# Attention on Trainium2: a home for the turned gate in the values' PSUM bank, and another place for it in the order

## Chip, cores, metric

The kernel runs on one core of one Trainium2 chip. The metric is the device time of one launch in microseconds (us).

## What is computed

One inference step of a two-layer hybrid encoder: a prompt of 1,024 tokens, and 8 running streams of 16 tokens each with caches. Each layer projects its input, runs three attention branches side by side (A: forgetting attention with a causal mask; B: a window of 128 tokens with sinks; C: latent attention with a mask by chunks of 64), multiplies each branch by silu of its gate, projects, merges and normalises. Cut to what matters here (prompt part, one layer):

```python
oa = _swept_attention(qa, ka, va, _causal, F)          # 8 heads of 64
ob = _banded_sink_attention(qb, kb, vb, sinks)
kc, vc = _mla_keys(ckv, kpe, w_uk, w_uv)
oc = _swept_attention(qc, kc, vc, _chunk_causal)
br = stack([oa * silu(ga), ob * silu(gb), oc * silu(gc)])
up = einsum('bsnw,nwd->bsnd', br, w_br)
mixed = (sigmoid(gates) * up).sum(axis=2)
```

The change is in the prompt's attention, and in `oa * silu(ga)` (and its like for B and C) there.

## The kernel before

Each layer runs phases one after the other, with a barrier of all engines between them. The phase of this change is `prompt_attention`. It works through 12 units: 4 pairs of heads for each of the kinds a, b and c. A unit has 16 sub-steps m; sub-step m takes head m % 2 of the pair and the 128 queries of tile a = m // 2. The window of tile a has a + 1 key tiles in kinds a and c, and at most two in kind b.

For one sub-step the engines do this:

- **Score** (PE, L1438, for kind a also the mask L1442): queries by keys into the PSUM tile `ss`. DVE then takes the row's maximum (L1558), and ACT the exponential into `p` (L1509), which also sums the rows.
- **Turn** (PE, L1452): the probabilities are transposed 128 columns at a time into `tr`, a ring of two PSUM banks. Up to four transposes make one group, and a group fills one bank. A sub-step with up to four key tiles (m up to 7 in kinds a and c, every m in kind b) has one group, later ones two. DVE copies the last group of a sub-step into `pt` (L1565), ACT the first of two (L1516). Behind the copy of an odd sub-step DVE divides the gate by the row sums (L1574, L1575) and writes it to `sgr`.
- **Value** (PE, L1469), once for both heads of a tile, behind the odd sub-step: values by `pt` into the PSUM bank `oo`, which holds the two heads' 128 x 128 result.
- **Gate** (PE, L1478): `sgr` is transposed, into the same ring `tr`, as a group of its own. **Mix** (DVE): the turned gate is copied to SBUF (L1581, `sgt`), and `oo` times `sgt` goes to `o` (L1586).
- **Fill** (PE, L1488 to L1490, 24 matmuls): a piece of the projection for the merge gates, put in between; ACT evicts it (L1523).

The order is one list, written out by `attention_order`; every engine walks it and does its own part. For an even m it reads: turn m, score m + 2, gate and mix of the tile before, perhaps a fill. For an odd m: turn m, score m + 2, perhaps a fill, value. (In kind b both scores m + 2 and m + 3 stand behind the even turn.) Fills stand at all odd m and at m = 4 in kinds a and b (m = 4 only in the last unit of b), and in kind c at m = 2, 3, 4, 5, 6, 8, 10, 12 and 13. With m + 2 past 15 the score is that of the next unit.

PE runs its instructions in order. `bank_free(pe, g)` holds group g of the ring until group g - 2 has been copied out. Since the gate is a group too, the groups of an odd turn with two groups go into the banks in this way: the even turn has g and g + 1, the gate g + 2, the odd turn g + 3 and g + 4; so g + 4 waits for the copy L1581 of the gate, which stands on DVE behind the maximum of score m + 2.

Of the kernel before, what the change touches and what calls it, by code (L numbers as in the profile page):

```python
# [14 lines left out]
P = 128  # L15
# [1103 lines left out]
def attention_order():  # L1119


    order = [("score", 0, 0), ("score", 0, 1)]
    fills = [(n, t) for n in range(len(UNITS)) for t in range(NT)][EARLY_FILLS:]
    order = [("fill", *fills.pop(0)) for _ in range(3)] + order
    places = {kind: [1, 3, 5, 7, 9, 11, 13, 15, 4] if kind != "c" else [2, 3, 4, 5, 6, 8, 10, 12, 13] for kind in "abc"}
    spare = EARLY_FILLS + 3
    for n in range(len(UNITS)):
        for m in range(SUBS):
            before = None if m % 2 or m + n == 0 else (n, m // 2 - 1) if m else (n - 1, PT - 1)
            order.append(("turn", n, m))  # L1130
            n2, m2 = (n, m + 2) if m + 2 < SUBS else (n + 1, m + 2 - SUBS)
            if n2 < len(UNITS) and UNITS[n2][0] != "b":
                order.append(("score", n2, m2))
            elif n2 < len(UNITS) and m2 % 2 == 0:
                order += [("score", n2, m2), ("score", n2, m2 + 1)]
            if before:
                order += [("gate", *before), ("mix", *before)]
            if m in places[UNITS[n][0]][:len(places["a"]) - (n < spare)]:
                order.append(("fill", *fills.pop(0)))
            if m % 2:  # L1140
                order.append(("value", n, m // 2))
    order += [("gate", len(UNITS) - 1, PT - 1), ("mix", len(UNITS) - 1, PT - 1)]
    assert not fills
    return order


def prompt_attention(nc, C, T, S, l):
# [33 lines left out]
    chain = ph.sem("chain")  # L1181
    tr_made, tr_taken = ph.sem("tr_made"), ph.ring("tr_taken", 2)
    s_made, max_ready, exp_ready = ph.sem("s_made"), ph.sem("max_ready"), ph.sem("exp_ready")
    sgr_ready, pv_made, o_ready = (ph.sem(n) for n in ("sgr_ready", "pv_made", "o_ready"))
    o_stored = ph.ring("o_stored", 2)
    gw_loaded, gw_hi, gw_lo = ph.sem("gw_loaded"), ph.sem("gw_hi"), ph.sem("gw_lo")
    g_made, g_taken, g_stored = ph.sem("g_made"), ph.sem("g_taken"), ph.ring("g_stored", GOUTS)
# [10 lines left out]
    for what, n, *of in order:  # L1198
        if what == "turn":
            first = len(groups_all(groups))  # L1200
            groups[what, n, *of] = [first + i for i in range(len(copied_groups(UNITS[n][0], of[0] // 2)))]
        elif what == "gate":
            groups[what, n, *of] = [len(groups_all(groups))]

    def bank_free(eng, g):

# [2 lines left out]

    def copied(eng, g):  # L1210
        eng.wait_ge(tr_taken[g % 2], g // 2 + 1)

    def sub(n, m):
        return SUBS * n + m
# [33 lines left out]
    with nc.Block() as block:  # L1248
# [171 lines left out]
        @block.tensor  # L1420
        def _(pe):
            def score(n, m):
                kind = UNITS[n][0]
                a, u, s, at = m // 2, m % 2, m % 2, aside(n, m)
                if a % 4 == 0:
                    for x in "kq":
                        stack_ready(pe, n, x, 0 if kind == "b" and x == "k" else u, a // 4)
                    pe.wait_ge(q_rows[a // 4], 16 * ("abc".index(kind) + 1))
                    pe.wait_ge(k_rows[n % 2], 16 * {"a": n // 2 + 1, "b": 3, "c": 4}[kind])
                if sub(n, m) >= earlier(n, m):  # L1430
                    pe.wait_ge(exp_ready, sub(n, m) - earlier(n, m) + 1)
                first, w = window(kind, a)[0] * P, len(window(kind, a)) * P
                stacks = {"x": kx[:, n % 2, 0 if kind == "b" else u], "y": ky[:, n % 2, 0 if kind == "b" else u]}
                queries = {"x": qx[:, u, rows(a)], "y": qy[:, u, rows(a)]}
                for c in range(0, w, 512):
                    cw = min(512, w - c)
                    for i, (q, k, depth) in enumerate(PASSES[kind]):
                        mm = nc.tensor.matmul(ss[:, s, at + c:at + c + cw], queries[q][0:depth], stacks[k][0:depth, first + c:first + c + cw],  # L1438
                                              start=i == 0, stop=i + 1 == len(PASSES[kind]) and (kind != "a" or c + cw < w),
                                              skip_group_check=True)  # L1440
                if kind == "a":
                    mm = nc.tensor.matmul(ss[:, s, w - P:w], C["ident16"][:], C["mask_a"][:], start=False, stop=True,  # L1442
                                          skip_group_check=True)
                mm.then_inc(s_made, 1)

            def turn(n, m):
                kind, at = UNITS[n][0], aside(n, m)
                pe.wait_ge(exp_ready, sub(n, m) + 1)
                for g, js in zip(groups["turn", n, m], copied_groups(kind, m // 2)):
                    bank_free(pe, g)  # L1450
                    for j in js:
                        mm = nc.tensor.transpose(tr[:, g % 2, (j % 4) * P:(j % 4 + 1) * P], p[:, m % 2, at + j * P:at + (j + 1) * P],  # L1452
                                                 C["ident"][:])
                    mm.then_inc(tr_made, 1)

            def value(n, a):
                kind = UNITS[n][0]
                for m in (2 * a, 2 * a + 1):
                    for g in groups["turn", n, m]:
                        copied(pe, g)  # L1460
                if a == 0:
                    pe.wait_ge(vs_loaded[n % 2], 32 * (n // 2 + 1))
                if PT * n + a:
                    pe.wait_ge(o_ready, PT * n + a)
                tiles = window(kind, a)
                for j, t in enumerate(tiles):
                    for u in range(2):
                        half = slice(u * HD, u * HD + HD)
                        mm = nc.tensor.matmul(oo[half, 0:P], v[:, n % 2, t, slice(0, HD) if kind == "b" else half],  # L1469
                                              pt[:, u, j * P:(j + 1) * P], start=j == 0, stop=j == len(tiles) - 1,  # L1470
                                              skip_group_check=True, tile_position=(0, u * HD))
                mm.then_inc(pv_made, 1)

            def gate(n, a):
                g = groups["gate", n, a][0]
                pe.wait_ge(sgr_ready, PT * n + a + 1)
                bank_free(pe, g)
                nc.tensor.transpose(tr[:, g % 2, 0:P], sgr[:], C["ident"][:]).then_inc(tr_made, 1)  # L1478

            def fill(n, t):  # L1480
                if t == 0:
                    pe.wait_ge(gw_lo, 2 * n)
                if fill_of(n, t):
                    pe.wait_ge(g_taken, fill_of(n, t))
                wh, wl = gate_weights(n)
                for k in range(KT):
                    hi, lo = (x[:, k, rows(t)] for x in (xh, xl))
                    nc.tensor.matmul(gacc[:, 0:GW], hi, wh[:, k, :], start=k == 0, stop=False)  # L1488
                    nc.tensor.matmul(gacc[:, 0:GW], hi, wl[:, k, :], start=False, stop=False)  # L1489
                    mm = nc.tensor.matmul(gacc[:, 0:GW], lo, wh[:, k, :], start=False, stop=k == KT - 1)  # L1490
                mm.then_inc(g_made, 1)

            for t in range(PT):
                mm = nc.tensor.transpose(ss[0:H, 0, rows(t)], C["fsum"][:, t, :], C["ident"][:])
            mm.then_inc(f_turned, 1)
            for what, *of in order:
                if what != "mix":
                    {"score": score, "turn": turn, "value": value, "gate": gate, "fill": fill}[what](*of)
# [49 lines left out]
        def _(dve):  # L1548
# [12 lines left out]
            def turn(n, m):  # L1561
# [5 lines left out]
                if m % 2:  # L1567
                    i, both = PT * n + a, slice((m - 1) % 4, m % 4 + 1)
                    if a == 0:
                        dve.wait_ge(vs_loaded[n % 2], 32 * (n // 2 + 1))  # L1570
                    if i >= 1:
                        dve.wait_ge(tr_made, groups["gate", (i - 1) // PT, (i - 1) % PT][0] + 1)
                    dve.wait_ge(exp_ready, sub(n, m) + 1)
                    ch.link(nc.vector.reciprocal(stat[:, both, 2:3], stat[:, both, 1:2]))  # L1574
                    nc.vector.tensor_tensor(heads_of(sgr[:], 2), heads_of(sg[:, n % 2, a, :], 2),  # L1575
                                            stat[:, both, 2:3].to_broadcast([P, 2, HD]), ALU.mult).then_inc(sgr_ready, 1)

            def mix(n, a):
                i, g = PT * n + a, groups["gate", n, a][0]
                dve.wait_ge(tr_made, g + 1)  # L1580
                nc.vector.tensor_copy(sgt[:], tr[:, g % 2, 0:P]).then_inc(tr_taken[g % 2], 1)  # L1581
                dve.wait_ge(pv_made, i + 1)
                copied(dve, g)
                if n:
                    dve.wait_ge(o_stored[a // 4], 16 * n)
                nc.vector.tensor_tensor(o[:, rows(a)], oo[:, 0:P], sgt[:], ALU.mult).then_inc(o_ready, 1)  # L1586

            dve.wait_ge(f_high, 1)
            ch.link(nc.vector.scalar_tensor_tensor(out=f_rest, in0=ss[0:H, 0, :], scalar=-1.0, in1=parts[0],
# [989 lines left out]
```

## Time and profile before

| | us |
|---|---|
| median of 3 runs | 3404.48 (3403.31 to 3406.72) |
| the profiled execution's own time | 3403.32 |
| its span, first to last instruction | 3401.6 |
| PE busy | 3092.8 (91% of the span) |
| DVE busy | 1439.0 (42%) |
| ACT busy | 875.4 (26%) |
| POOL busy | 540.9 (16%) |

PE is TensorE with its matmuls and PEld its weight loads, DVE is VectorE, ACT ScalarE, POOL GpSimd. The busy time of an engine is the sum of its instructions' durations where they do not overlap. Matmuls are pipelined: the time from one start to the next is shorter than the duration that a row gives, so a stall of PE is read from starts and not from the idle time alone. Rows of a timeline merge like instructions that follow one another (x4 is four of them), and show in brackets the idle time before the first and what ended it.

### The profile page before, as it was taken

What the parts mean: (1) busy time and instruction counts of PE and PEld (TensorE: products, weight loads), DVE (VectorE), ACT (ScalarE), POOL (GpSimd) and SP (SyncE); (2) the same over time, 40 slices, a digit from 0 to 9 for tenths busy, and PEclk for the clock granted to TensorE, in tenths of its full rate; (3) what the DMA queues carried; (4) which work ended last, traced back from release to release, by engine and by line L of the source; (5) the groups of instructions that cost most, each with busy time, mean ns of one, the idle gap of its engine ahead of it and who ended that gap; (6) DMA issues with size and microseconds to landing.
All of it is one profiled execution on the core that took longest, in us unless ns stands there. A gap on an engine that the chain in (4) does not pass through costs nothing. (4 is left out here: it accounts for less than half of the span.)

```text
span 3401.6 us, 52390 instructions
## 1 busy us (share of the span) xinstructions
PE 3092.8 (91%) x20340; PEld 2619.3 (77%) x20340; DVE 1439.0 (42%) x3224; ACT 875.4 (26%) x1997; POOL 540.9 (16%) x503
## 2 busy tenths in 40 slices
PE   1999998799999996889989999987999999788988
PEld 1888887688888884677768888876888888655877
DVE  6214233344554442354642142343445544334555
ACT  2211122233323331220221212233333233222110
POOL 2000000144344310000000000003433543000000
PEclk9999999899999997899999999998999999898999
DMA  5432315534343418573543322154424432286534
GB/s 197 143 114 79 100 59 164 147 83 116 99 135 89 111 35 234 176 245 139 191 132 126 95 90 81 55 187 123 117 77 121 137 106 70 76 263 233 188 126 147
DMA packets 331825, 442.66 MB, mean 130 GB/s; under 512 B 62180, under 2 KB 226404, under 8 KB 329068
## 3 DMA queue, kind: packets, MB, share of 16 engines
q1 hardware_dynamic: 304036, 404.48, 38.7%
q10 hardware_dynamic: 27536, 34.74, 3.2%
q8 instruction: 166, 2.72, 0.3%
q14 instruction: 87, 0.71, 0.1%
HBM read 310.64 MB, written 131.27 MB: 130 GB/s over the span
## 5 line engine op out<-in xcount | busy, mean ns | idle before, releaser
L503 PE MATMUL proj_acc<-proj_wh,keep_xh 128*128 128x512 f32 (+1 forms) x1152 | 449.9, 391 | 1.2 <-DVE proj_wl L432 1.2
L505 PE MATMUL proj_acc<-proj_wh,keep_xl 128*128 128x512 f32 (+1 forms) x1152 | 444.7, 386 | 0.0
L504 PE MATMUL proj_acc<-proj_wl,keep_xh 128*128 128x512 f32 (+1 forms) x1152 | 444.1, 386 | 0.0
L1565 DVE COPY att_pt<-att_tr 128x256 f32<-128x256 f32 (+3 forms) x384 | 177.1, 461 | 580.1 <-PE att_tr L1452 579.0
L1509 ACT ACTIVATE att_p<-att_ss,att_stat 128x257 f32<-128x257 f32 (+9 forms) x384 | 249.4, 650 | 524.6 <-DVE att_stat L1558 442.1
L1558 DVE TENSOR_REDUCE att_stat<-att_ss 128x1 f32<-128x257 f32 (+9 forms) x384 | 245.2, 639 | 61.1 <-PE att_ss L1438 29.2
L1452 PE MATMUL att_tr<-keep_ident,att_p 128*128 128x128 f32 x1392 | 235.3, 284 | 34.9 <-DVE att_sgt L1581 19.8
L1488 PE MATMUL att_gacc<-att_gw,keep_xh 128*128 128x256 f32 x864 | 251.2, 291 | 0.6 <-ACT att_gout L1523 0.6
L1488 PE MATMUL att_gacc<-keep_gw,keep_xh 128*128 128x256 f32 x800 | 237.5, 297 | 13.0 <-ACT att_gout L1523 13.0
L503 PEld LDWEIGHTS proj_acc<-proj_wh,keep_xh 128*128 128x128 f32 x1152 | 216.9, 188 | 41.1 <-DVE keep_xl L589 1.8
L505 PEld LDWEIGHTS proj_acc<-proj_wh,keep_xl 128*128 128x128 f32 x1152 | 216.8, 188 | 41.0
L504 PEld LDWEIGHTS proj_acc<-proj_wl,keep_xh 128*128 128x128 f32 x1152 | 217.1, 188 | 38.4
L1490 PE MATMUL att_gacc<-att_gw,keep_xl 128*128 128x256 f32 x864 | 243.7, 282 | 0.0
L1489 PE MATMUL att_gacc<-att_gw,keep_xh 128*128 128x256 f32 x864 | 243.4, 282 | 0.0
L1489 PE MATMUL att_gacc<-keep_gw,keep_xh 128*128 128x256 f32 x800 | 229.3, 287 | 0.0
L1490 PE MATMUL att_gacc<-keep_gw,keep_xl 128*128 128x256 f32 x800 | 228.8, 286 | 0.0
L1452 PEld LDWEIGHTS att_tr<-keep_ident,att_p 128*128 128x128 f32 x1392 | 151.1, 141 | 94.4 <-issue 58.5
L1469 PE MATMUL att_oo<-att_pt,att_v 128*64 128x128 f32 x2784 | 194.4, 279 | 10.8 <-DVE att_pt L1565 10.8
L2260 PE MATMUL up_acc<-up_wh,up_bh 128*128 128x512 f32 x432 | 172.7, 400 | 30.5 <-DVE up_bl L2300 30.5
L1438 PE MATMUL att_ss<-att_kx,att_qx 128*128 128x256 f32 (+7 forms) x512 | 190.7, 378 | 4.1 <-DMA att_ky<-scratch_forget 4.1
L1469 PEld LDWEIGHTS att_oo<-att_pt,att_v 128*64 128x64 f32 x2784 | 148.5, 136 | 37.6 <-DVE att_pt L1565 13.3
L2261 PE MATMUL up_acc<-up_wl,up_bh 128*128 128x512 f32 x432 | 171.6, 397 | 0.0
(342 smaller groups left out, 6194.0 us busy)
## 6 DMA issues: line engine op xcount, KB each, us to landing
up_gates<-scratch_gates SPq DMA_DIRECT2D x18, 1536.0 KB, 7.9
scratch_gates<-att_gout SPq DMA_DIRECT2D x208, 128.0 KB, 1.7
att_graw<-in_w_in SPq DMA_DIRECT2D x44, 512.0 KB, 4.1
keep_early<-in_w_in SPq DMA_DIRECT2D x40, 512.0 KB, 3.7
str_ka<-in_cache_a_kT SPq DMA_DIRECT2D x16, 1024.0 KB, 8.4
str_va<-in_cache_a_v SPq DMA_DIRECT2D x16, 1024.0 KB, 5.4
scratch_sg<-proj_out SPq DMA_DIRECT2D x54, 256.0 KB, 2.1
att_sg<-scratch_sg SPq DMA_DIRECT2D x24, 512.0 KB, 6.2
```

Source lines behind the costliest of these rows:

```text
L503: nc.tensor.matmul(bank, hi, mh, start=kt == 0, stop=False)
L504: nc.tensor.matmul(bank, hi, ml, start=False, stop=False)
L505: mm = nc.tensor.matmul(bank, lo, mh, start=False, stop=kt == KT - 1)
L1438: mm = nc.tensor.matmul(ss[:, s, at + c:at + c + cw], queries[q][0:depth], stacks[k][0:depth, first + c:first + c + cw], start=i == 0, sto ...
L1452: mm = nc.tensor.transpose(tr[:, g % 2, (j % 4) * P:(j % 4 + 1) * P], p[:, m % 2, at + j * P:at + (j + 1) * P], C["ident"][:])
L1469: mm = nc.tensor.matmul(oo[half, 0:P], v[:, n % 2, t, slice(0, HD) if kind == "b" else half], pt[:, u, j * P:(j + 1) * P], start=j == 0, s ...
L1488: nc.tensor.matmul(gacc[:, 0:GW], hi, wh[:, k, :], start=k == 0, stop=False)
L1489: nc.tensor.matmul(gacc[:, 0:GW], hi, wl[:, k, :], start=False, stop=False)
L1490: mm = nc.tensor.matmul(gacc[:, 0:GW], lo, wh[:, k, :], start=False, stop=k == KT - 1)
L1509: nc.scalar.activation(p[:, s, place], ss[:, s, place], ACT.Exp, bias=stat[:, m % 4, 0:1], accum_out=stat[:, m % 4, 1:2]).then_inc(exp_rea ...
L1558: nc.vector.tensor_reduce(stat[:, m % 4, 0:1], ss[:, s, at:at + w + (kind == "b")], AXX, ALU.max, negate=True)\
L1565: nc.vector.tensor_copy(pt[:, m % 2, js[0] * P:(js[-1] + 1) * P], tr[:, g % 2, 0:len(js) * P])\
```

## The change

The gate's transpose leaves the ring `tr`. The bank `oo` now holds two tiles of results, each with 128 columns of values and 128 columns of turned gate; tile a uses half a % 2. The gate signals with a semaphore of its own, `sg_turned`. Gate and value of a tile wait until the mix of the tile two before is done, where value waited for the mix of the tile before. And in the order the gate's transpose moves from behind score m + 2 to directly behind the turn of the even sub-step m; the mix stays where it was. No computation is added or removed.

```diff
             order.append(("turn", n, m))
+            if before:
+                order.append(("gate", *before))
             n2, m2 = (n, m + 2) if m + 2 < SUBS else (n + 1, m + 2 - SUBS)
...
             if before:
-                order += [("gate", *before), ("mix", *before)]
+                order.append(("mix", *before))
...
-        elif what == "gate":
-            groups[what, n, *of] = [len(groups_all(groups))]
...
+    def values_at(n, a):
+        return oo[:, 256 * (a % 2):256 * (a % 2) + P]
+
+    def gate_at(n, a):
+        return oo[:, 256 * (a % 2) + P:256 * (a % 2) + 2 * P]
...
-                if PT * n + a:
-                    pe.wait_ge(o_ready, PT * n + a)
+                if PT * n + a >= 2:
+                    pe.wait_ge(o_ready, PT * n + a - 1)
...
             def gate(n, a):
-                g = groups["gate", n, a][0]
                 pe.wait_ge(sgr_ready, PT * n + a + 1)
-                bank_free(pe, g)
-                nc.tensor.transpose(tr[:, g % 2, 0:P], sgr[:], C["ident"][:]).then_inc(tr_made, 1)
+                if PT * n + a >= 2:
+                    pe.wait_ge(o_ready, PT * n + a - 1)
+                nc.tensor.transpose(gate_at(n, a), sgr[:], C["ident"][:]).then_inc(sg_turned, 1)
...
             def mix(n, a):
-                i, g = PT * n + a, groups["gate", n, a][0]
-                dve.wait_ge(tr_made, g + 1)
-                nc.vector.tensor_copy(sgt[:], tr[:, g % 2, 0:P]).then_inc(tr_taken[g % 2], 1)
+                i = PT * n + a
+                dve.wait_ge(sg_turned, i + 1)
+                ch.link(nc.vector.tensor_copy(sgt[:], gate_at(n, a)))
                 dve.wait_ge(pv_made, i + 1)
-                copied(dve, g)
...
-                nc.vector.tensor_tensor(o[:, rows(a)], oo[:, 0:P], sgt[:], ALU.mult).then_inc(o_ready, 1)
+                nc.vector.tensor_tensor(o[:, rows(a)], values_at(n, a), sgt[:], ALU.mult).then_inc(o_ready, 1)
```

The wait of DVE's odd turn on the gate's transpose, before it overwrites `sgr`, is the same wait on the new semaphore.

## Rows read from the trace of the kernel before

**Rows 1.** The page: busy us, share of the span and instructions of each engine.

```profile
PE 3092.8 (91%) x20340; PEld 2619.3 (77%) x20340; DVE 1439.0 (42%) x3224; ACT 875.4 (26%) x1997; POOL 540.9 (16%) x503
```

**Rows 2.** Busy time by stretch: the attention phases of both layers, their sum.

```profile
sum 1285.00, PE 1221.29 PEld 1094.76 DVE 614.07 ACT 428.32 POOL 486.03; mean PE 610.65 PEld 547.38 DVE 307.03 ACT 214.16 POOL 243.02
```

**Rows 3.** Who waited for whom: us in total, times, longest.

```profile
PE att_tr L1452 <- DVE att_sgt L1581: 19.8, 26, 1.0
PE att_oo L1469 <- DVE att_pt L1565: 10.8, 16, 1.0
PE att_tr L1452 <- DVE att_pt L1565: 4.1, 18, 0.2
PE att_tr L1478 <- ACT att_pt L1516: 2.2, 5, 0.8
PEld att_tr L1452 <- issue: 58.5, 293, 0.4
```

**Rows 4.** Timeline: kind a, gate and odd turn with two groups (tile 6).

```profile
815.17 0.28 PE L1478 MATMUL att_tr<-keep_ident,att_sgr 128*128 128x128 f32 x1
815.29 0.60 PE L1452 MATMUL att_tr<-keep_ident,att_p 128*128 128x128 f32 x4
815.38 1.23 DVE L1558 TENSOR_REDUCE att_stat<-att_ss 128x1 f32<-128x1024 f32 x1 [0.45 <-PE att_ss L1442]
816.52 0.28 DVE L1581 COPY att_sgt<-att_tr 128x128 f32<-128x128 f32 x1
816.85 0.55 PE L1452 MATMUL att_tr<-keep_ident,att_p 128*128 128x128 f32 x3 [0.96 <-DVE att_sgt L1581]
817.44 0.56 DVE L1565 COPY att_pt<-att_tr 128x384 f32<-128x384 f32 x1 [0.26 <-PE att_tr L1452]
821.24 1.75 PE L1469 MATMUL att_oo<-att_pt,att_v 128*64 128x128 f32 x28
```

**Rows 5.** Timeline: kind a, gate and odd turn with one group (m = 5).

```profile
784.35 0.56 DVE L1565 COPY att_pt<-att_tr 128x384 f32<-128x384 f32 x1 [2.66 <-PE att_tr L1452]
784.70 0.28 PE L1478 MATMUL att_tr<-keep_ident,att_sgr 128*128 128x128 f32 x1
785.05 0.52 PE L1452 MATMUL att_tr<-keep_ident,att_p 128*128 128x128 f32 x3
```

**Rows 6.** Timeline: the same in kind b (m = 3).

```profile
892.95 0.42 DVE L1565 COPY att_pt<-att_tr 128x256 f32<-128x256 f32 x1 [1.82 <-PE att_tr L1452]
893.23 0.27 PE L1478 MATMUL att_tr<-keep_ident,att_sgr 128*128 128x128 f32 x1
893.52 0.41 PE L1452 MATMUL att_tr<-keep_ident,att_p 128*128 128x128 f32 x2
```

**Rows 7.** Timeline: kind c, end of a unit (m = 14 and 15).

```profile
1100.36 0.69 DVE L1565 COPY att_pt<-att_tr 128x512 f32<-128x512 f32 x1 [4.35 <-PE att_tr L1452]
1100.66 0.30 PE L1478 MATMUL att_tr<-keep_ident,att_sgr 128*128 128x128 f32 x1
1101.19 1.07 PE L1452 MATMUL att_tr<-keep_ident,att_p 128*128 128x128 f32 x8 [0.23 <-DVE att_pt L1565]
1101.53 0.29 DVE L1586 TENSOR_TENSOR att_o<-att_oo,att_sgt 128x128 f32<-128x128 f32 x1
1102.30 0.69 DVE L1565 COPY att_pt<-att_tr 128x512 f32<-128x512 f32 x1 [0.47 <-PE att_tr L1452]
1103.24 1.97 PE L1469 MATMUL att_oo<-att_pt,att_v 128*64 128x128 f32 x32 [0.69 <-DVE att_pt L1565]
```

**Rows 8.** Timeline: kind c, a gate behind ACT's copy (m = 8).

```profile
1193.66 0.59 ACT L1516 ACTIVATE att_pt<-att_tr 128x512 f32<-128x512 f32 x1
1194.39 0.30 PE L1478 MATMUL att_tr<-keep_ident,att_sgr 128*128 128x128 f32 x1 [0.83 <-ACT att_pt L1516]
```

**Rows 9.** Timeline: kind c, the scaled gate and the next even turn (m = 2).

```profile
1107.19 0.29 DVE L1575 TENSOR_TENSOR att_sgr<-att_sg,att_stat 128x128 f32<-128x128 f32 x1
1107.55 0.44 PE L1452 MATMUL att_tr<-keep_ident,att_p 128*128 128x128 f32 x2
```

More of the change, by code:

```diff
@@ L1183, in prompt_attention @@
     s_made, max_ready, exp_ready = ph.sem("s_made"), ph.sem("max_ready"), ph.sem("exp_ready")
-    sgr_ready, pv_made, o_ready = (ph.sem(n) for n in ("sgr_ready", "pv_made", "o_ready"))
+    sgr_ready, sg_turned, pv_made, o_ready = (ph.sem(n) for n in ("sgr_ready", "sg_turned", "pv_made", "o_ready"))
     o_stored = ph.ring("o_stored", 2)
@@ L1468, in value @@
                         half = slice(u * HD, u * HD + HD)
-                        mm = nc.tensor.matmul(oo[half, 0:P], v[:, n % 2, t, slice(0, HD) if kind == "b" else half],
+                        mm = nc.tensor.matmul(values_at(n, a)[half], v[:, n % 2, t, slice(0, HD) if kind == "b" else half],
                                               pt[:, u, j * P:(j + 1) * P], start=j == 0, stop=j == len(tiles) - 1,
@@ L1570, in turn @@
                         dve.wait_ge(vs_loaded[n % 2], 32 * (n // 2 + 1))
-                    if i >= 1:
-                        dve.wait_ge(tr_made, groups["gate", (i - 1) // PT, (i - 1) % PT][0] + 1)
+                    if i:
+                        dve.wait_ge(sg_turned, i)
                     dve.wait_ge(exp_ready, sub(n, m) + 1)
```

## Prediction

> **What bounds the kernel now.** I began with the page, then took the busy times of the two attention phases, then the list of waits, and read timelines around the gate. PE is busy for 91% of the whole span [rows 1]. In the two attention phases, 1285.0 us together, it is busy 1221.3 us, which is 95%, against 48% for DVE, 33% for ACT and 38% for POOL [rows 2]. So these phases last as long as PE's queue, and what counts is each moment at which PE stands still. The list of waits names four in this phase that the change can touch: the odd turn behind the gate's copy, 19.8 us in 26 times; the turn behind DVE's copy, 4.1 us; the gate behind ACT's copy, 2.2 us; and value behind DVE's copy, 10.8 us [rows 3]. The weight loads of the turns show another 58.5 us in 293 pieces of 0.2 us without a named releaser [rows 3]. Because the ends of matmuls are modelled and overlap, I take every loss from start to start instead. The reference is tile 6: the gate starts at 815.17 and the odd turn behind it at 815.29, so 0.12 us is the spacing where nothing is waited for, though the odd turn has waits of its own there; within a run of four transposes it is (0.60 - 0.27) / 3 = 0.11 us [rows 4].
>
> **The ring without the gate, odd turns with two groups (kind a, tiles 4 to 6).** The first four transposes start at 815.29, so the fifth is due at 815.74. It starts at 816.85, just behind the gate's copy (816.52 to 816.80), which stands on DVE behind the 1.23 us maximum [rows 4]. That is 1.11 us lost. Tiles 5 and 4, read the same way, lose 0.98 and 0.78. The figures repeat within 0.02 us in all 4 units of kind a and in both layers: 24 cases, 4 x (1.11 + 0.98 + 0.78) = 11.5 us per layer, **23.0 us**. After the change the second group needs the bank that the even turn's last group left, copied long before. What is late next? DVE still does maximum, gate copy and mix first, and starts its copy into `pt` at about 817.2 instead of 817.44. Value is what needs it; it starts at 821.24 and the copy ends at 818.00, 3.2 us earlier, because score and a fill stand between [rows 4]. So value can move up by the whole 1.1 us. Without that fill, only DVE's 0.2 us would be won.
>
> **The ring without the gate, odd turns with one group.** Here the gate pushes the odd turn into the bank of the even turn just before it, and it must wait for that copy. In kind a the copy ends at 784.91 and the turn starts at 785.05, 0.35 us behind the gate instead of 0.12: 0.23 lost [rows 5]. In kind b the copy ends at 893.37, the turn starts at 893.52, 0.29 behind the gate: 0.17 lost [rows 6]. After the change it needs the bank of the turn before that, which has long been copied. There are 15 such cases per layer in kind a (0.19 to 0.25 each, 3.3 us) and 23 in kind b (3.9 us), with 0.2 us in others: 7.4 us per layer, **14.8 us**. A fill stands before each of their values too.
>
> **Ends of units (m = 14 and 15).** The next unit's score is short, so DVE's copy of turn 14 is the late one: gate at 1100.66, turn 15 at 1101.19, 0.41 us over the reference [rows 7]; the gate was itself 0.2 us late behind ACT's copy in the same way. After the change both banks still have to be copied, the first by ACT and the second by DVE, so I keep 0.47 for a unit end inside kind a (3 per layer). The end from a to b also has a 0.44 us wait for the gate's copy: 0.91. In kind b it is 0.25 three times and 0.37 once. In kind c there is no fill behind turn 15, and value waits for DVE's copy: that copy can begin when the mix ends at 1101.82 instead of 1102.30, so 0.48 is won (3 per layer) [rows 7]. For the last unit I take 0.5, an estimate by the same rows. Per layer 1.4 + 0.9 + 1.1 + 1.4 + 0.5 = 5.3 us, **10.6 us** in all.
>
> **Gates behind ACT's copy in kind c.** At m = 8 the gate waits for ACT's copy, which ends at 1194.25, and starts at 1194.39 [rows 8], 1.0 us behind its due time; two others in that layer lose 0.6 and 0.2, one in the other layer 0.3. A fill follows there, not a turn, so nothing else needs that bank at once: **2.2 us** won.
>
> **The gate's new place.** Nothing is added: the 192 transposes cost 0.11 to 0.12 us of PE each in either place. Behind the gate now stand the score m + 2, and through it the maximum and the exponential, 0.12 us later. That is covered wherever a fill follows. At m = 0 and 1 of kind c no fill does, and value 0 waits for DVE, whose work goes through that maximum: 8 x 0.12 = **0.9 us lost**. The gate's own wait is for `sgr`. The tightest common case is m = 2 of kind c: `sgr` is written at 1107.48 and the second transpose of the turn starts at 1107.66, so the gate is due at 1107.78, 0.3 us behind it [rows 9]. In all other places a longer value or a fill lies between. I take nothing for it. The looser wait of value costs and gives nothing: value already waits for the odd copy, which DVE makes behind the mix (817.44 in rows 4), so the mix of the tile before is always done.
>
> The shared bank deserves one look. DVE reads the values and the gate from `oo` during the mix, and PE's next write there is the value at 821.24, 3.2 us behind the copy that itself follows the mix [rows 4]. The Trainium skill (PSUM — Partial Sum Buffer, section on bank collisions) says that PE writing and DVE reading one bank at the same time raise an error and are not arbitrated, and advises a different bank for what is read. That speaks against two tiles in one bank if they are to overlap; by the rows they never do, and the sum would be the same.
>
> **Sum.** 23.0 + 14.8 + 10.6 + 2.2 - 0.9 = 49.7 us. The profiled execution took 3403.3 us (its span 3401.6, 1.7 around it), so 3353.6; the median of the runs lies 1.2 above it: about **3355 us**, 1.5% less.
>
> **Rivals.**
> - *The short gaps are a fixed price (0.13).* The 0.17 to 0.25 us before one-group turns may be no copy wait but what starting a turn costs, as the 58.5 us in 293 pieces suggest: some of these stand before turns that wait for nothing [rows 3]. Against it, tile 6 starts its odd turn at 0.12 behind the same gate [rows 4], and in rows 5 and 6 the turn follows the end of the copy by 0.14 and 0.15. Then 14.8 us stay: 3370 us.
> - *The stall moves (0.08).* PE arrives earlier and waits elsewhere, for DVE's copy or ACT's exponential, as value does in kind c (0.69 us in rows 7). With DVE only 0.24 us earlier per two-group turn, 24 x 0.24 = 5.8 us are left of 23.0, so 3355 + 17 = 3372, and to about 3385 if the one-group turns fare the same. Against it stand the fill and DVE's 48% [rows 2, 4].
> - *Nothing to see (0.03).* Moves and stalls cancel within 0.2%, 3398 to 3411 us.
> - *The gate blocks PE (0.04).* `sgr` comes late at the new place, with score m + 2 queued behind, where it used to be in front. It costs from the moment that the average gate waits 49.7 / 192 = 0.26 us; at 0.5 us each, 96 us are lost and 50 won: 3450 us. For it: one slack is only 0.3 us [rows 9]. Against it: everywhere else value or fill lies between.
>
> **How the numbers follow.** The forecast has 0.72, with 3346 to 3363 as its own range: 1.5 us more for the restart of transposes after a stall and the turns at m = 1 of kind c at the low end, estimated unit ends at nothing at the high one. With the first rival and the lower part of the second the range is 3345 to 3376, and about 1.7 in 10 is left out. 0.2% is 6.8 us, about what a measurement can tell. Faster: 0.72 + 0.13 + 0.08 = 0.93; within: 0.03; slower: 0.04.
>
> **What would show it.** The turn's wait on L1581 is gone from the list of waits; two-group odd turns appear as one row of x5 to x7; the odd turn follows the score at 0.12 us in kinds a and b; a unit of kind a is 57.1 us long before and should be about 4.2 us shorter, one of kind b about 1.3; value's waits on DVE's copy stay at their count of 16 or so, those of kind c. Wrong would be: new idle time before the gate on L1575, a longer wait of value, or a gap of 0.2 us that now stands before the one-group turns although the copy was long done.

## The result, and the profile after

| | before | after |
|---|---|---|
| median of the runs, us | 3404.78 (3403.31 to 3406.72, 4 runs) | 3344.59 (3343.30 to 3347.76, 4 runs) |
| ratio, 95% interval | 1 | 0.9829 (0.9817 to 0.9842) |
| time of the profiled execution, its span | 3403.32, 3401.6 | 3347.76, 3346.1 |

The change makes the kernel 1.7% faster. The forecast was 3355 us, with a range of 3345 to 3376; this median lies 0.4 us below its low end, and two later ones of the same kernel (3347.78 and 3348.38, below) lie inside. One execution of a later version took 6074.4 us against 3330 to 3334 for its five others, and is left out there. The profiled execution of after is the slowest of its four, so the traces show a difference of 55.6 us where the medians show 60.2.

The page of the kernel after, and its busy times by stretch over the two attention phases, which answer to [rows 1, 2]:

```profile
span 3346.1 us, 52386 instructions
PE 3062.3 (92%) x20340; PEld 2618.5 (78%) x20340; DVE 1440.7 (43%) x3224; ACT 872.1 (26%) x1997; POOL 540.7 (16%) x503
```

```profile
sum 1233.00, PE 1195.28 PEld 1096.62 DVE 614.00 ACT 425.11 POOL 486.86; mean PE 597.64 PEld 548.31 DVE 307.00 ACT 212.56 POOL 243.43
```

The same instructions run on PE, and DVE's busy time in the stretches is unchanged (614.1 and 614.0 us). The stretches around the two phases are 1233 us long instead of 1285, and PE is busy for 97% of them instead of 95%. That PE's own busy time also falls, by 26 us, I read as a matter of reckoning, which no run isolates: a row's duration is longer than the spacing, so the transpose before a stall counts in full. In [rows 5] the gate counts 0.28 us where 0.12 is its spacing, and so hides 0.16 of the 0.23 us lost behind it.

The list of waits after, PE's part that belongs to attention, answers to [rows 3] (us in total, times, longest). The turn is now L1458, value L1475, the gate L1484:

```profile
PE att_gacc L1494 <- ACT att_gout L1529: 13.6, 8, 4.3
...
PE att_tr L1458 <- ACT att_p L1515: 9.4, 2, 5.0
...
PE att_oo L1475 <- issue: 6.5, 8, 0.8
...
PE att_oo L1475 <- DVE att_pt L1571: 6.2, 8, 1.0
...
PE att_ss L1444 <- POOL att_qy L1394: 1.2, 2, 0.9
...
PE att_tr L1458 <- ACT att_pt L1522: 1.1, 4, 0.3
```

and in the list of all engines:

```profile
PEld att_tr L1458 <- issue: 34.3, 194, 0.4
```

The turn's waits for the gate's copy and for DVE's copy are gone, and so is the gate's for ACT's copy. Value keeps its 16 waits, all in kind c, of which the profile now labels 8 "issue". No wait stands before the gate. The short pieces without a named releaser at the turns' weight loads are 99 fewer, and 24 us less, than in [rows 3]. One wait is new: twice PE now waits for POOL, which prepares queries for the scores of kind c (`att_qy`). The list of before has no such row.

The timeline after at tile 6 of the same unit as in [rows 4] (excerpt):

```profile
806.93 0.23 PE L1448 MATMUL att_ss<-keep_mask_a,keep_ident 128*128 128x128 bf16 x1
807.00 0.93 PE L1458 MATMUL att_tr<-keep_ident,att_p 128*128 128x128 f32 x7
807.20 1.23 DVE L1564 TENSOR_REDUCE att_stat<-att_ss 128x1 f32<-128x1024 f32 x1 [0.57 <-PE att_ss L1448]
807.69 0.48 PE L1444 MATMUL att_ss<-att_kx,att_qx 128*128 128x512 f32 x1
808.34 0.28 DVE L1587 COPY att_sgt<-att_oo 128x128 f32<-128x128 f32 x1
808.87 0.55 DVE L1571 COPY att_pt<-att_tr 128x384 f32<-128x384 f32 x1
811.77 1.75 PE L1475 MATMUL att_oo<-att_pt,att_v 128*64 128x128 f32 x28
```

All seven transposes of the odd turn stand in one row, 0.07 us behind the mask. The gate's copy on DVE is where it was, behind the 1.23 us maximum; nothing on PE waits for it any more. The copy into `pt` ends at 809.42, and value starts at 811.77: 2.35 us are left of the 3.2.

A finer measure than the span comes from the starts of the mix (L1586, then L1591): the time from the first mix of one unit to that of the next. Units are numbered from 0. Layer 1, in us, from one trace of each kernel:

| | kind a, units 1 and 2 | kind b, units 4 to 6 | b to c | kind c, units 8 to 10 |
|---|---|---|---|---|
| before | 57.14, 57.11 | 38.10, 38.10, 38.20 | 39.38 | 60.91, 60.20, 61.47 |
| after | 52.48, 52.50 | 36.57, 36.62, 36.59 | 38.68 | 59.96, 59.65, 59.96 |

From first to last mix of each layer, both layers together, attention takes 1255.7 us before and 1200.8 after; all the rest of the span takes 2145.9 and 2145.3.

### The profile page after: what moved, and what is told of

It reads as the page before. It is cut to its first block and busy times, and to the rows that moved or that the text cites. A ratio compares the mean times of both kernels' runs of the same rounds, so it can differ in the third digit from the quotient of the medians.

```text
span 3346.1 us, 52386 instructions
## 1 busy us (share of the span) xinstructions
PE 3062.3 (92%) x20340; PEld 2618.5 (78%) x20340; DVE 1440.7 (43%) x3224; ACT 872.1 (26%) x1997; POOL 540.7 (16%) x503
## 5 line engine op out<-in xcount | busy, mean ns | idle before, releaser
L1458 PE MATMUL att_tr<-keep_ident,att_p 128*128 128x128 f32 x1392 | 227.7, 282 | 10.5 <-ACT att_p L1515 9.4
L1475 PE MATMUL att_oo<-att_pt,att_v 128*64 128x128 f32 x2784 | 194.4, 279 | 12.7 <-issue 6.5
L1458 PEld LDWEIGHTS att_tr<-keep_ident,att_p 128*128 128x128 f32 x1392 | 152.3, 141 | 45.6 <-issue 34.3
L1475 PEld LDWEIGHTS att_oo<-att_pt,att_v 128*64 128x64 f32 x2784 | 148.5, 136 | 39.2 <-issue 9.9
L1396 POOL CAST att_kx<-keep_early 128x512 fp32r<-128x512 f32 x44 | 27.0, 613 | 895.7 <-POOLq L115 869.5
```

What stands on the lines that cost most here:

```text
L1475: mm = nc.tensor.matmul(values_at(n, a)[half], v[:, n % 2, t, slice(0, HD) if kind == "b" else half], pt[:, u, j * P:(j + 1) * P], start=j ...
```

## The experiments

Attention's time below is always that from first to last mix, both layers, in the one profiled execution.

**The changed kernel again.**

> The changed kernel once more, on the same chip as the three beside it. In one profiled execution of each, the two attention phases account for 54.9 us of the gain, while the medians differ by 60. If the rest is chance between executions, this one's median lies between 3344 and 3350 us against 3405 before; if something outside attention became faster too, it stays at 60 us gained and shows in the stretches outside attention again.

Measured: median 3347.78, ratio 0.9817 (0.9803 to 0.9831), where before took 3409.06 beside it. Attention 1201.0 us, the rest 2151.0. Attention repeats within 0.2 us, which is partly chance, since the first unit of layer 1 differs by 1.2 us (58.26 and 59.50) and others make up for it. The rest does not repeat: it is 5.7 us longer than in the first trace.

**Only the home.** In the changed kernel the gate's transpose goes back behind the score:

```diff
             order.append(("turn", n, m))
-            if before:
-                order.append(("gate", *before))
...
             if before:
-                order.append(("mix", *before))
+                order += [("gate", *before), ("mix", *before)]
```

> The gate has its home in the values' bank, but its transpose stays behind score m + 2, as before the change. Theory (the gain comes from the ring alone, the place in the order is neutral): the same as the changed kernel within 2 us, if anything about 1 us faster, since the scores of kind c start 0.12 us earlier where value 0 waits for DVE. Rival (the new place carries part of the gain): at least 5 us slower than the changed kernel.

Measured: 3348.40, ratio 0.9827 (0.9803 to 0.9850); attention 1200.7 us against 1200.8 and 1201.0. The timeline of this kernel at tile 6 (its turn is L1456, its gate L1482) shows the gate back between mask and turn, at the price of one transpose:

```profile
803.44 0.23 PE L1446 MATMUL att_ss<-keep_mask_a,keep_ident 128*128 128x128 bf16 x1
803.51 0.28 PE L1482 MATMUL att_oo<-keep_ident,att_sgr 128*128 128x128 f32 x1
803.63 0.93 PE L1456 MATMUL att_tr<-keep_ident,att_p 128*128 128x128 f32 x7
```

The home alone carries the whole gain, within what the traces can tell; the rival that the place has a share in it falls. Units 8 to 10 of kind c take 59.70, 59.71 and 59.69 us, on average 0.16 less than with the move, near the 0.12 that the prediction gave for value 0 of such a unit. In the sum that is lost in the scatter.

**Only the move.** In the kernel before, with the gate still in the ring:

```diff
             order.append(("turn", n, m))
+            if before:
+                order.append(("gate", *before))
...
-                order += [("gate", *before), ("mix", *before)]
+                order.append(("mix", *before))
```

> The gate stays in the ring, only its transpose moves directly behind the even turn. Theory: with two groups in the even turn the gate now waits at once for ACT's copy of the first of them, with the score queued behind it: about 0.5 to 0.85 us at four tiles of each of 8 units, 22 us per layer, and the odd turn's wait for the gate's copy stays: 44 us slower than before, near 3449 us. Rival (place carries the gain): faster than before. Rival (the place is neutral also in the ring): within 5 us of before.

Measured: 3459.0, ratio 1.0150 (1.0132 to 1.0168), 50 us slower than before; attention 1308.7 us, 53 more than in before's first trace. The list of waits of this kernel (gate L1480, turn L1454):

```profile
PE att_tr L1480 <- ACT att_pt L1518: 38.6, 64, 1.9
PE att_tr L1454 <- DVE att_sgt L1583: 23.5, 26, 1.1
```

and its timeline at tile 6:

```profile
821.46 0.98 PE L1454 MATMUL att_tr<-keep_ident,att_p 128*128 128x128 f32 x7
822.15 0.60 ACT L1518 ACTIVATE att_pt<-att_tr 128x512 f32<-128x512 f32 x1 [0.74 <-PE att_tr L1454]
...
822.89 0.30 PE L1480 MATMUL att_tr<-keep_ident,att_sgr 128*128 128x128 f32 x1 [0.45 <-ACT att_pt L1518]
824.05 0.61 PE L1454 MATMUL att_tr<-keep_ident,att_p 128*128 128x128 f32 x4
```

The 64 waits are those of four tiles in 8 units of both layers. The gate needs the bank that ACT is only starting to empty at 822.15, and holds up the score behind it. So the move is harmless only with the new home, and it is not neutral by itself. It came out 6 us dearer than the 44 expected, and 9 or more by attention's time.

**One tile in the bank, strict waits.**

```diff
     def values_at(n, a):
-        return oo[:, 256 * (a % 2):256 * (a % 2) + P]
+        return oo[:, 0:P]
     def gate_at(n, a):
-        return oo[:, 256 * (a % 2) + P:256 * (a % 2) + 2 * P]
+        return oo[:, P:2 * P]
...
-                if PT * n + a >= 2:
-                    pe.wait_ge(o_ready, PT * n + a - 1)
+                if PT * n + a:
+                    pe.wait_ge(o_ready, PT * n + a)
```

(the last in value and in gate).

> Like the changed kernel, but with one tile in the bank (128 columns of values, 128 of gate) and the strict wait: gate and value of a tile wait for the mix of the tile just before. Theory (mix always precedes the odd copy on DVE, so the second tile frees nothing): the same as the changed kernel within 2 us. Rival (two tiles are needed to keep PE from waiting): slower by at least 0.1 us per value, 19 us or more.

Measured: 3346.64, ratio 0.9820 (0.9805 to 0.9835). Units 1 and 2 take 52.49 and 52.49 us, those of kind b 36.57, 36.62, 36.58, those of kind c 59.96, 59.64, 59.96: the changed kernel's figures within 0.01. Attention is 1195.5 us, 5 less, but 4.4 of that lie in the first unit of each layer (55.29 and 57.03 us against 58.26 and 58.42), where PE waits for a fill's eviction, and that wait differs between executions (2.9 us at the longest here, 4.3 in the trace of after). The second tile buys nothing.

**The gate ahead of the turn.**

```diff
-            order.append(("turn", n, m))
             if before:
                 order.append(("gate", *before))
+            order.append(("turn", n, m))
```

> The changed kernel with the gate one place further ahead: in front of the even turn, directly behind value. This uses up the slack against the scaled gate. Theory (value and fill cover the making of it nearly everywhere): only the gate at m = 2 of kind c waits, about 0.1 to 0.2 us in 8 units, 1 to 2 us slower than the changed kernel. Rival (the gate blocks PE as soon as it comes early): 0.26 us or more per gate, 50 us, so back at the time of before.

Measured: 3352.98, ratio 0.9851 (0.9829 to 0.9872); attention 1204.3 us, 3.5 more. Its list of waits:

```profile
PE att_oo L1484 <- DVE att_sgr L1581: 1.0, 2, 0.8
```

Two gates in 192 wait long enough to be listed, and both stand in kind b, not at m = 2 of kind c as expected. Units 1 and 2 take 52.64 and 52.58 us, about 0.1 more, and those of kind c about 0.1 more too. Of the 3.5 us, 2.8 lie in the one stretch from b to c of layer 1 (41.49 us against 38.68), where PE also waits 1.4 us for POOL's queries, as it does in the changed kernel. The median is 5 to 8 us above those of the changed kernel in its own comparisons; the intervals of the ratios overlap, so I can't say that more than the 1 to 2 us expected is lost. Of the 50 us of the rival nothing is to be seen: even directly behind value, the gate does not block PE.

**Kind c's fills at the odd sub-steps.**

```diff
-    places = {kind: [1, 3, 5, 7, 9, 11, 13, 15, 4] if kind != "c" else [2, 3, 4, 5, 6, 8, 10, 12, 13] for kind in "abc"}
+    places = {kind: [1, 3, 5, 7, 9, 11, 13, 15, 4] if kind != "c" else [1, 3, 5, 7, 9, 11, 13, 15, 4] for kind in "abc"}
```

> The changed kernel with kind c's fills where kind a has them (all odd m, and m = 4), so that a fill stands in front of every value. Theory (what is left of waits in kind c is value behind DVE's copy at m = 1 and m = 15, 0.8 and 0.7 us in each unit, and a fill covers it): about 12 us faster than the changed kernel, 3333 us. Rival (the fills at even m were covering something else, such as the odd turn behind ACT's copy): the same or slower.

> The changed kernel with kind c's fills at the odd m, once more, on one chip with the two beside it: 3334 us, 1190 us of it in attention.

Measured: 3334.31 and, in a second comparison, 3332.30 (five executions); ratios to before 0.9789 (0.9772 to 0.9806) and 0.9787 (0.9768 to 0.9807). Attention takes 1190.2 and 1187.8 us. Units 8 to 10 of kind c fall to 58.28, 58.10 and 58.29 us, while the stretch from b to c grows by 2 to 3 us, since a fill now stands before that mix, and the last unit becomes 3.9 us shorter. Together that is some 6 us per layer, near the 12 us expected in all. The list of PE's waits has no row of value any more. In the changed kernel, value 0 of a unit of kind c starts so (timeline, PE only):

```profile
1085.01 0.28 PE L1444 MATMUL att_ss<-att_kx,att_qy 96*128 96x256 f32 x1
1086.10 0.44 PE L1475 MATMUL att_oo<-att_pt,att_v 128*64 128x128 f32 x4 [0.81 <-issue]
```

PE stands for 0.81 us between the score and the value; with the fill in that gap there is no such bracket. This version is the fastest of the study, with or without the move. The rest of the span took 2140.6 us in the second trace, the least of all.

**The same fills in the kernel before.**

> The kernel before with the same places for kind c's fills. Theory: it wins the same 12 us at m = 1 and 15, but opens the wait of the odd turn for the gate's copy at tiles 4, 5 and 6 of kind c, as in kind a, about 2.9 us per unit and 23 us in all, and 0.2 us at each one-group turn, 5 us: about 15 us slower than before. Rival (kind c has no such wait): faster than before by about 12 us.

Measured: 3416.4, ratio 1.0036 (1.0023 to 1.0049), 12 us slower than before; attention 1266.5 us, 11 to 15 more than in the two traces of before. Its list of waits:

```profile
PE att_tr L1452 <- DVE att_sgt L1581: 39.9, 50, 1.0
```

The wait for the gate's copy has gone from 26 times to 50: 24 more are the three tiles of the four units of kind c in two layers. In the kernel before, kind c's fills at even m hid this stall and paid for it with value's; with the gate out of the ring that bargain is no longer needed.

**Before again, and the two best beside the changed kernel.**

> The kernel before once more, for a second profiled execution of it. Attention took 1255.7 us in its first trace (first mix to last mix of each layer) and the rest 2145.9. If the difference between the medians (60 us) and attention's share of it in the traces (55 us) is chance, attention again takes 1255 to 1257 us and the rest anything from 2145 to 2151 us, as in the traces of the changed kernels; if the change also helps outside attention, the rest is well above 2151 us here.

Measured: 3403.10, ratio 1.0001 (0.9986 to 1.0015); attention 1251.5 us, the rest 2144.0. Attention is 4 us shorter than in the first trace, for the most part in the first unit of each layer (61.36 and 62.67 us against 63.96 and 63.55), so it did not repeat within the 1255 to 1257 us expected. The rest is at the low end: no sign that the change helped anything outside attention.

> Home in the values' bank, the gate's transpose left at its old place, and kind c's fills at the odd m. Theory (place neutral): within 2 us of the same kernel with the gate moved, 3334 us, with units of kind c of 58.2 us. Rival (the new place pays once value no longer waits): 5 us or more slower than it.

Measured: 3333.39, ratio 0.9794 (0.9773 to 0.9815), units of kind c of 58.23, 58.08 and 58.24 us. Attention is 1184.5 us, 3 to 6 less than with the move; of this 3 to 5 us lie in the first unit of layer 2 (54.99 us, where the two traces with the move have 59.92 and 57.75), which scatters anyway. The place of the gate pays nothing here either.

> The changed kernel as it is, for comparison with the two versions with moved fills on the same chip: 3345 to 3348 us, 1201 us of it in attention.

Measured: 3348.38, ratio 0.9833 (0.9812 to 0.9855); attention 1199.3, the rest 2147.4.

## Why the prediction was right, and where its sizes were off

The mechanism was right in nearly every term; the sum was some 10 us too small against the medians. Three traces of the changed kernel give 1200.8, 1201.0 and 1199.3 us for attention, two of before 1255.7 and 1251.5, so attention gained 53.2 us on average, and 54.9 between the first two traces, where the sum had 49.7.

Measured from the first transpose of each even turn to that of the next, averaged over these two traces of before and three of after, both layers, in us:

| term | forecast | measured |
|---|---|---|
| odd turns with two groups | 23.0 | 25.3 |
| odd turns with one group | 14.8 | 17.2 |
| ends of units | 10.6 | 9.2 |
| gates behind ACT's copy | 2.2 | 1.8 |
| new place, and all else in kind c | -0.9 | -0.4 |
| sum | 49.7 | 53.1 |

That the sum came within 4 us owes something to luck: two terms were too small, and one, the ends of units, held a part that did not happen at all.

**Odd turns with two groups.** Forecast 0.78, 0.98 and 1.11 us. From the even turn of a tile to the even turn of the next, the traces show 8.01, 8.82 and 9.58 us before, in the unit of [rows 4], and 7.09, 7.73 and 8.40 after: 0.92, 1.09 and 1.18. Over 24 cases that is 25.5 us in place of 23.0. The part mis-sized is above all the restart: behind a stall the row of three transposes took 0.55 us where 0.49 is the spacing's share. That is 1.5 us over 24 cases, and I named it but put it into the range instead of the sum. About 1 us more is spread over hundredths that I can't place. The copy into `pt` now has less slack before value, as forecast, and it suffices: no value in kinds a and b waits. So the second rival, that the stall moves, falls for these turns.

**Odd turns with one group.** Here the first rival said that the short gap is a fixed price. It falls. In kind b the turn now starts 0.12 us behind the score, where [rows 6] had a gate and 0.29 us (timeline of after, m = 1 of the first unit):

```profile
873.56 0.33 PE L1458 MATMUL att_tr<-keep_ident,att_p 128*128 128x128 f32 x1
873.72 0.27 PE L1484 MATMUL att_oo<-keep_ident,att_sgr 128*128 128x128 f32 x1
873.75 0.37 PE L1444 MATMUL att_ss<-att_kx,att_qx 128*128 128x256 f32 x1
...
874.19 0.28 PE L1444 MATMUL att_ss<-att_ky,att_qy 80*128 80x256 f32 x1
...
874.31 0.27 PE L1458 MATMUL att_tr<-keep_ident,att_p 128*128 128x128 f32 x1
```

A unit of kind b became 1.5 us shorter and not 1.3, each step by 0.20 us instead of 0.17. A unit of kind a became 4.6 us shorter, forecast 4.2. The restart is missing here as well: in [rows 6] the row of two transposes behind the short stall takes 0.41 us, and after the change the same row takes 0.38 (at 878.62). Over some 76 such turns, 0.03 us each make up most of the 2.4 us by which the term was too small.

**Ends of units.** Inside kinds a and b an end gained 0.49 and 0.27 us, forecast 0.47 and mostly 0.25, and in kind c 0.50, forecast 0.48. From b to c, where 0.37 was forecast, it lost 0.5 on average. There the second rival came true on a small scale: PE arrives earlier at the first scores of kind c and waits for POOL, which prepares their queries (`att_qy`), 1.2, 0.9 and 2.1 us in all in the three traces of after; in the two of before no such wait is listed. The prediction named POOL only with its 38% of busy time. The longer wait of layer 2 (timeline of after, PE only):

```profile
2659.32 0.30 PE L1444 MATMUL att_ss<-att_kx,att_qx 104*128 104x128 f32 x1 [0.93 <-POOL att_qy L1394]
```

In kind c the gain at m = 15 is the DVE's, as forecast. The timeline after answers to [rows 7]:

```profile
1080.04 1.10 PE L1458 MATMUL att_tr<-keep_ident,att_p 128*128 128x128 f32 x8
...
1080.86 0.29 DVE L1591 TENSOR_TENSOR att_o<-att_oo,att_sgt 128x128 f32<-128x128 f32 x1
...
1081.17 0.69 DVE L1571 COPY att_pt<-att_tr 128x512 f32<-128x512 f32 x1
```

The copy follows the mix at once: from the mix's start to the copy's start it is 0.31 us, where [rows 7] had 0.77. That is 0.46, and 0.48 was forecast.

**Gates behind ACT's copy.** They start on time now, and gained 1.8 us by the average; the 2.2 forecast came from one trace, and the second trace of before lists 1.3 us in 3 such waits where the first had 2.2 in 5. At the place of [rows 8] the gate stands at 1170.85, right behind the turn, while ACT's copy begins only at 1171.87 (timeline of after):

```profile
1170.85 0.27 PE L1484 MATMUL att_oo<-keep_ident,att_sgr 128*128 128x128 f32 x1
...
1171.87 0.59 ACT L1522 ACTIVATE att_pt<-att_tr 128x512 f32<-128x512 f32 x1
```

In the ring it would have had to wait for that copy to end, and that is what "only the move" pays for.

**The new place.** I took nothing for it but 0.9 us in kind c, and that holds: "only the home" has the same attention time within 0.3 us, and its units of kind c are 0.16 us shorter. The slack at m = 2 of kind c, put at 0.3 us, is 0.26 to 0.35 in the trace of after, and 0.26 is the least of all 192 gates. The rival that the gate blocks PE has not happened, and not even one place further ahead.

**The shared bank.** The prediction counted 3.2 us between DVE's last read of `oo` and PE's next write there, from tile 6. The tightest place is narrower: at m = 1 of kind c the mix ends at 1085.80 and value starts at 1086.10, 0.30 us later (trace of after; the least in that of before is 0.30 too). No row of PE that writes `oo` overlaps a row of DVE that reads it, in any trace of these kernels. What keeps the two apart is the order and not the distance: value waits for DVE's copy into `pt`, which stands behind the mix on DVE.

**What stays open.** The medians gained 60.2 us in the first comparison; in the other two it is 61.3 and 57.4 us. That is a few more than attention's 53 to 55. The intervals of the three ratios reach from 49 to 67 us. The rest of the span scatters from 2140.6 to 2151.0 us between profiled executions of all these kernels, without order between those with and without the change, and the first unit of a layer scatters by some 3 us too. So I can't tell whether a few us were gained elsewhere.

## What to carry to other kernels

In a ring of buffers, look at who empties each slot and what that engine does first. A small tenant emptied late (here one transpose whose copy stood behind a 1.2 us reduction) holds up the large ones, and a ring of two turns every such lateness into a stall. Free columns of a bank that already has a fitting order of writers and readers are a home at no cost. Read stalls from start to start, and count the short ones: 0.2 us, mostly without a named releaser, 38 times a layer, was more than a quarter of this gain. When PE gets faster, look too at engines that were never late before, as POOL here. And after a stall is gone, look for work that had been placed to hide it: moving the fills afterwards gave another 0.4%, in an order that made the kernel before slower.

## What I had not expected of the hardware

At its new place the gate's transpose starts 0.16 us behind the turn, and the score only 0.03 us behind the gate (873.56, 873.72, 873.75). In the trace of before the score started 0.09 us behind such a turn without a gate (888.19, 888.28). So the gate costs PE 0.10 us here and 0.11 to 0.12 at its old place, only divided otherwise.

A run of transposes that restarts behind a long stall has 0.17 us between its first two starts (816.85 and 817.02) instead of 0.11, and so loses 0.06 us more than the stall itself. This is not peculiar to a stall: every even turn that follows value directly shows the same 0.16 to 0.17 us, though PE waited for nothing (168 turns of the trace of before, and 168 of after).
